# Zero rows under the transposed queries and keys: products over 128 rows in retention, banded and latent attention

## The reference, cut to what matters

```python
# retention, 4 heads of 64, per chunk of 64 tokens
s = einsum('bnihd,bnjhd->bnhij', qc, kc) * d_intra
# banded attention with a sink, 4 query heads and 2 key heads of 64, band of 128 tokens
s = einsum('bnikgd,bnjkd->bnkgij', qc, kb) * 64 ** -0.5
# latent attention, 4 heads of 64 + 32 = 96, causal by chunks of 64
s = einsum('bqhd,bkhd->bhqk', q_blk, k) * 96 ** -0.5
```

## Time and profile before

| | |
|---|---|
| median of 3 runs | 4515.14 us (4513.99 to 4517.41) |
| profiled execution, its own time | 4508.02 us |
| its span in the trace | 4506.2 us |
| mean granted TensorE clock | 0.954 |
| PE busy | 4199.6 us (93%) |
| DVE, ACT, POOL busy | 58%, 34%, 46% |
| the section `mixers` | 206 to 358 us in layer 0, 2451 to 2598 us in layer 1 |

### The profile page before, as it was taken

One profiled execution on the slowest core, in us unless ns is written; L12 is line 12 of the kernel. 1 busy time (PEld: TensorE's weight loads), 2 busy tenths in 40 slices (PEclk: granted clock), 3 DMA queues, 4 the chain that ended last, 5 costly groups with the idle time before them and its releaser, 6 DMA issues. The chain is left out here.

```text
span 4506.2 us, 57623 instructions
## 1 busy us (share of the span) xinstructions
PE 4199.6 (93%) x18760; PEld 3405.9 (76%) x18760; DVE 2624.7 (58%) x5086; ACT 1515.2 (34%) x2741; POOL 2062.1 (46%) x1270
## 2 busy tenths in 40 slices
PE   6797889999999999999977878899999999999999
PEld 5365777878888788888863657788888887888887
DVE  6664330887686455555567634318776864555554
ACT  3244333334333322222232433334343333222222
POOL 7402523556465544444373025336465555444443
PEclk9967999999999999999989679999999999999999
DMA  3102314475664866666421023244755748666664
GB/s 108 39 1 80 103 54 129 135 209 169 182 199 145 260 191 193 195 191 192 139 94 35 1 82 100 64 134 142 205 175 166 213 144 256 192 194 195 189 193 140
DMA packets 504914, 656.66 MB, mean 146 GB/s; under 512 B 293856, under 2 KB 299104, under 8 KB 501600
## 3 DMA queue, kind: packets, MB, share of 16 engines
q1 hardware_dynamic: 203616, 519.45, 36.1%
q10 hardware_dynamic: 301056, 134.24, 10.8%
HBM read 508.88 MB, written 144.70 MB: 145 GB/s over the span
## 5 line engine op out<-in xcount | busy, mean ns | idle before, releaser
L1752 DVE TENSOR_TENSOR t_hots<-t_stages,t_hots 128x512 fp32r<-128x512 f32 x256 | 620.8, 2425 | 604.7 <-ACT t_hots L1566 604.7
L1605 POOL TENSOR_TENSOR t_ul<-t_u,t_uh 128x1024 fp32r<-128x1024 f32 x252 | 608.9, 2417 | 577.9 <-ACT t_uh L1507 577.9
L1777 PE MATMUL bank<-h_high,t_uh 128*128 128x512 f32 x2048 | 805.6, 393 | 26.1 <-ACTq L1574 12.7
L1777 PE MATMUL bank<-h_low,t_uh 128*128 128x512 f32 x2048 | 803.1, 392 | 0.0
L1777 PE MATMUL bank<-h_high,t_ul 128*128 128x512 f32 x2048 | 800.0, 391 | 0.0
L1819 PE MATMUL bank<-t_v_early,t_hots 128*128 128x512 f32 x3072 | 711.9, 391 | 12.1 <-DVE t_hots L1752 12.1
L1819 PE MATMUL bank<-h_high,t_hots 128*128 128x512 f32 x3072 | 706.7, 389 | 0.0
L1819 PEld LDWEIGHTS bank<-t_v_early,t_hots 128*128 128x128 f32 x3072 | 580.1, 189 | 133.8 <-DVE t_hots L1752 12.9
L1819 PEld LDWEIGHTS bank<-h_high,t_hots 128*128 128x128 f32 x3072 | 576.6, 188 | 119.7
L1622 POOL TENSOR_TENSOR t_v_early<-t_stages,t_v_early 128x1024 fp32r<-128x1024 f32 x128 | 306.7, 2396 | 392.8 <-ACT t_v_early L1562 392.8
L1622 POOL TENSOR_TENSOR h_high<-t_stages,h_high 128x1024 fp32r<-128x1024 f32 x128 | 308.1, 2408 | 380.0 <-ACT h_high L1562 380.0
(11 more groups left out here) (386 smaller groups left out, 6250.2 us busy)
## 6 DMA issues: line engine op xcount, KB each, us to landing
t_u<-in_peer_u SPq DMA_DIRECT2D x256, 512.0 KB, 3.6
t_stages<-in_peer_v SPq DMA_DIRECT2D x256, 512.0 KB, 4.1
acts<-t_act ACTq DMA_DIRECT2D x256, 256.0 KB, 3.1
gates<-t_stages ACTq DMA_DIRECT2D x128, 512.0 KB, 5.6
t_stages<-acts SPq DMA_DIRECT2D x256, 256.0 KB, 4.2
t_stages<-gates SPq DMA_DIRECT2D x256, 256.0 KB, 4.5
p_w_raw<-in_peer_wq SPq DMA_DIRECT2D x64, 256.0 KB, 3.1
m_w_raw<-in_w_in SPq DMA_DIRECT2D x48, 256.0 KB, 2.6
```

The costliest lines, as they stand in the source:

```text
L1605: e.tensor_tensor(ul[:, n % 2, :, :], u[:, n % 2, :, :], uh[:, n % 2, :, :].bitcast(F32), ALU.subtract).then_inc(u_split, 1)
L1752: e.tensor_tensor(al[:, s, :], a_in[:, s, :], ah[:, s, :].bitcast(F32), ALU.subtract).then_inc(act_split, 1)
L1777: mm = e.matmul(k.bank[n % 2][:, :], a[:, n % 2, q, :], b[:, q, :], start=(q == 0 and m == 0), stop=(q == KT - 1 and m == 2))
```

## The change

The tiles `turned` and `wT` get 128 rows in place of 96 and 64. GpSimd gets a program with two memsets that write zeros to rows 64 to 127 of both, once per layer. Scores are then products over all 128 rows. ScalarE's copies write the same rows as before (latent heads overwrite the zeros in rows 64 to 95). TensorE waits for both memsets ahead of `J_RT`.

```diff
+        lat_ready, win_ready, ..., sink_ready, lat_squared, zeroed = k.sems[:21]
...
-        turned = sb("turned", [MD, 2 * NH, SEQ])
-        rT, mT = turned[0:HD, :, :], turned[:, :, :]
+        turned = sb("turned", [P, 2 * NH, SEQ])
+        rT = mT = turned
...
-        wT = sb("wT", [HD, NW, SEQ])
+        wT = sb("wT", [P, NW, SEQ])
...
+            @block.gpsimd
+            def _(e):
+                e.memset(turned[HD:P, :, :], 0.0).then_inc(zeroed, 1)
+                e.memset(wT[HD:P, :, :], 0.0).then_inc(zeroed, 1)
...
-                    e.activation(rT[:, n - J_RT, :], k.bank[n % 8][0:HD, :], ACT.Copy).then_inc(scalar_freed, 1)
+                    e.activation(rT[0:HD, n - J_RT, :], k.bank[n % 8][0:HD, :], ACT.Copy).then_inc(scalar_freed, 1)
...
-                    e.activation(wT[:, n - J_WIN, :], k.bank[n % 8][0:HD, :], ACT.Copy).then_inc(scalar_freed, 1)
+                    e.activation(wT[0:HD, n - J_WIN, :], k.bank[n % 8][0:HD, :], ACT.Copy).then_inc(scalar_freed, 1)
...
-                    e.activation(mT[:, n - J_FULL, :], k.bank[n % 8][0:MD, :], ACT.Copy).then_inc(scalar_freed, 1)
+                    e.activation(mT[0:MD, n - J_FULL, :], k.bank[n % 8][0:MD, :], ACT.Copy).then_inc(scalar_freed, 1)
...
                 e.wait_ge(rows_ready, 1)
+                e.wait_ge(zeroed, 2)
                 for n in range(J_RT, J_RS):
```

More of the change, by code:

```diff
@@ L693, in mixers @@
     p_loaded, w_loaded, m_loaded, pe_jobs, vec, vector_freed, scalar_freed, to_root, rooted, squares_made, rows_ready, \
-        lat_ready, win_ready, q_ready, keys_ready, silu_ready, s_ready, p_ready, sink_ready, lat_squared = k.sems[:20]
+        lat_ready, win_ready, q_ready, keys_ready, silu_ready, s_ready, p_ready, sink_ready, lat_squared, zeroed = k.sems[:21]
     J_LAT, J_UP, J_RT, J_RS, J_WIN, J_RV, J_FULL, base = 0, 3, 11, 19, 35, 41, 45, 53
```

## The result

| | before | after |
|---|---|---|
| median | 4514.57 us (4506.82 to 4517.41, 4 runs) | 4476.25 us (4473.44 to 4481.28, 4 runs) |
| ratio, 95% interval | | 0.9918 [0.9904, 0.9933] |
| mean granted clock | 0.954 | 0.966 |

The account below looks back on a forecast made before the run. PE at half its clock was taken to set the section's pace. Gains 2 x (3.0 + 4.8 + 3.4) + 5.5 = 27.9 us, less 6 for memsets, gave 22 us: 4515.1 to 4493 us, range 4480 to 4514.

Parts of the forecast that it names:

- all 64-row products: Reading of the profile before: with 64 rows, retention's scores and banded units have PE busy at clock 0.50.
- Banded: Banded units of attention: 25.3 us where 32 stand; with a late clock rise 4.8 us per layer, switch included.
- Latent: Latent units of attention: first ones 15.6 for 19 us, 3.4 per layer; last ones 5.5 us in layer 0 only.
- the factor: Any stretch that VectorE bounds: its length is taken as VectorE's busy time times 1.10.
- the low start that had been allowed for: Start of the banded units: PE has gaps until 284, clock rises by 290, so 23 of 32 us profit.
- the switch of rows: Between 64-row scores and other products in banded steps: 0.38 us per full step, 4.0 us per layer, 8 in all.
- the two slower rivals: The rivals that the clock ignores rows (4513 us, chance 0.14) or doesn't hold in banded units (4501 us, 0.16).
- so I charge 3.0 us per layer: Section's start: memsets hold VectorE's L789 to 213.3, delaying all behind it; 6 us in all, bounds 0 and 13 per layer.
- retention, 3.0 us per layer: Retention's scores: full rows raise the clock by 252 to 254, saving 3.0 us per layer; bounds 0 and 4.
- The clock doesn't follow the rows: Rival for the whole section: only the switch goes, 8 us gained and 6 charged, 4513 us; chance 0.14.
- It doesn't hold in the banded units: Rival: the clock rises but may fall back in banded units, gain there near 4.0 us; 4501 us, chance 0.16.
- Long memsets: Rival, L788 to L801: memsets hold VectorE 13 us per layer, 26 us in all; 4513 us, chance 0.10.

Follow-up runs that it names:

- the three profiles: The change itself against the kernel before, profiled and timed three times: 4476.25, 4479.51 and 4479.13 us, ratios 0.9918, 0.9942 and 0.9937.
- the three other profiles: Kernel before with padded tiles and memsets alone, with only retention's scores over 128 rows, and with banded scores over 96 rows: ratios 1.0001, 0.9978 and 0.9993.
- the 96-row kernel: Banded scores over 96 rows, retention 64 and latent 96 as in the kernel before: ratio 0.9993 to that kernel.
- the longer version: The changed kernel with three more memsets of `turned` ahead, each with its own wait: 0.9978 of the kernel before, where the change has 0.9942.
- The repeated comparisons: The unaltered changed kernel timed twice more against the kernel before: 4479.51 us, 0.9942, and 4479.13 us, 0.9937.

## Why the prediction was right and wrong

The prediction read too much into retention in one point: "all 64-row products" at 0.50 was its second batch; the first, over 64 rows too, ran at 1.00.

**Right in size: attention.** Banded 9.3, 9.5 and 9.5 us over both layers in the three profiles, 9.6 forecast. Latent 11.8, 11.2 and 11.4, forecast 2 x 3.4 + 5.5 = 12.3; by layer 9.6 and 2.2 in the first profile, for 8.9 and 3.4. These gains are counted from 85.7 us in the one profile of before; the three other profiles with 96 rows and a low clock at entry had 86.6, 81.9 and 82.8, so part of the agreement is luck. VectorE did take over the pace, at a factor a little above 1.10: at the upper clock it is busy for 5.26 of 6.00 us of banded steps (294 to 300 us), so 1.14. The stage took 26.1 to 28.0 us, 25.3 by the factor alone and 27.2 with the low start that had been allowed for.

**Mis-sized within it: the switch of rows.** 2.0 us per layer by the 96-row kernel, not 4.0. This left the sum alone, as it was contained in the 4.8, but it was also the floor of the two slower rivals, which should have stood 4 us higher.

**Wrong: the term "so I charge 3.0 us per layer" for the memsets.** This is the step that failed, 6 of the 22 us. The mechanism is there (3.58 us in the longer version); its place was not. Memset elements take 3.51 / 4096 = 0.86 ns, not 1.0, and L789 (L794 now) did not wait for both memsets: it got in between them, done at 205.53. The second ended at 208.13, 0.15 us before VectorE's next instruction of the kind that a memset holds (L801 of the changed kernel, at 208.28). The step counted both memsets as one block that VectorE could not enter; what it charged with 3.0 us measured 0. Without this charge the same sum gives 27.9 us, the section's 27.9 to 30.1, and 4487 from the 4515.14 taken. That the 27.9 is met so closely is luck: in the first profile retention gained 6.4 us more than its term, and the stage ahead of it lost 5.3.

**Mis-sized: retention, 3.0 us per layer.** It measured 12.4, 10.7 and 9.4 us over both layers where 6.0 stood. The sum let the clock fall in the 3.25 us wait ahead of the second batch and rise again by 254. In four of six layers it did not fall at all (7.0 us); in the others it did, and they gained 4.7 and 3.4. The stage before, up to that batch, took 5.3, 2.2 and 0.2 us more than in the profile of before; it has two or three lengths (42.4 to 43.1, or 45) in kernels with and without the change, so it is a matter of when the clock rose, and I had no term for it.

**Outside the sum.** 27.9 to 30.1 us against 38 measured: 4 to 7 are the four runs of the kernel before, and what the profiles show outside the section varies over 4195 to 4217 us with no order in it. So of the 16 us between 22 and 38, the memsets are 6; the other 10 lie outside the section, 4 to 7 of them in the few runs of the kernel before, and the cause of the rest stays open. The repeated comparisons, 26 and 28 us, agree with the section.

**The rivals.** "The clock doesn't follow the rows" (4513) falls; its point that chance has a part in when the clock rises stands. "It doesn't hold in the banded units" was half seen: it was low for 6 to 20 us at their start, and fell again in some (0.72 in layer 1), at a cost of 0.5 to 1.9 us against the 26.1 of the best. Long memsets: none.

## What to carry to other kernels

The gain ends where the next engine takes over, here at VectorE's busy time by about 1.14. When GpSimd work is added beside VectorE, charge each blocked instruction by the one GpSimd instruction that it meets, and read from the timeline which gap each falls in; only where many blocked instructions follow one another, as with the longer memsets, does the delay come near the sum.

## What the runs showed of the hardware that was not expected

- Rows count by degree: in retention (512-column products) 96 rows raise the clock and 64 do not; in banded attention, with 64-column value products between, 96 do not and 128 do.
- Full rows are not a guarantee: 128-row latent steps ran at 0.50 for nearly 14 us with PE busy for 13.88 of 14.00.
- A batch of 64-row products keeps the upper clock while it lasts (4.55 us, as with 128 rows), but in 12 of 12 layers the clock was low behind the 3.25 us wait that follows, against 5 of 12 with 128 rows.
- The clock can be lost to short gaps as well as to a long one: with the 5.3 us wait filled it still fell at 272 us, among waits of 0.4 to 0.8 us.
- GpSimd's memset of 64 x 4096 float32 takes 3.51 us, of 64 x 3072 2.69 us, against 4.92 us for 128 x 2048 with two inputs.
